# State-space blocks in a hybrid encoder: decay sums spread to all partitions by adding transfers instead of matmuls

## The chip, the core and the metric

The kernel runs on one core of a Trainium2 chip. The metric is the device time of one execution in microseconds (us). Before the change its median is 2278.6 us over 3 runs (2277.65 to 2280.53).

## What is computed

Two layers of an encoder are applied to two groups of tokens, 256 and 512 (768 tokens together), with width 1024. Each layer has a mixer (a Hyena convolution beside a Mamba-2 state-space scan), cross-attention into memory, and an MLP. The change lies in the state-space part of the mixer alone. What it must compute for each chunk of 128 tokens, cut to what matters:

```python
def segsum_exp(a):
    cs = jnp.cumsum(a, axis=-1)
    diff = cs[..., :, None] - cs[..., None, :]
    return jnp.where(mask, jnp.exp(jnp.where(mask, diff, 0.0)), 0.0)

Lmat = segsum_exp(dA)                               # per head, chunk and direction: 128 x 128
cb = jnp.einsum("bclgn,bcsgn->bgcls", Cc, Bc)       # per group of heads and chunk: 128 x 128
y_diag = jnp.einsum("bgrcls,bcsgrp->bclgrp", cb[:, :, None] * Lmat, xd)
```

There are 8 heads in 2 groups and 6 chunks of 128 tokens, so 12 blocks in a layer (block n: chunk n // 2, group n % 2). For each block and each of the two directions, the kernel needs exp(cs[l] - cs[s] + mask) for 4 heads: a tile of 128 partitions (s) by 4 x 128 (l). The term cs[l] must therefore stand on every partition: that is what "spread" means here.

## The kernel before, in words

Everything is in feature-major layout: 128 features on the partitions, 768 tokens along the row. All weights come from one stream of chunks in DRAM, 128 x 1024 each. TensorE works on float32 data as three products of rounded halves (high x high, low x high, high x low). A weight chunk is prepared by three engines: SyncE loads `raw`, ScalarE writes `wlo` = -raw and `whi` = rounded raw (`high_part`, L686 and L687), and GpSimd issues a DMA that adds the chunk from DRAM onto `wlo` (`low_halves`, L635). This is done in two halves of 512 columns. Each weight slot is used by every second tile.

The input projection is a run of 20 tiles per layer (`project(j)` on TensorE, through `tile`, L1346). A tile is 8 steps k of 6 matmuls, each over 384 tokens. A hook can put other products between two steps. Tiles 0 to 7 give the inputs of the scan, tiles 8 to 19 those of Hyena. Beside tiles 8 to 19 the 12 state-space blocks are worked, one beside each tile, in an order that each engine's own program writes out by hand:

- TensorE: `turn_cum` (L1452) transposes the cumulated sums after tile 8. `blocks(n)` writes C.B of the block into bank `MB[0]` (L1266) and, for both directions, the spread cs[l] into `MB[2]` and `MB[3]`: a matmul of a column of `group_r`, broadcast, against `wide` (L1271, and L1274 for block 0), added onto the mask that ScalarE laid into the bank. Block 0 has its mask from a matmul with `mask_r` (L1275). `blocks(0)` is in the middle of tile 9 (hook at k = 4), `blocks(n)` after tile 8+n. `diag(n)` (L1286, 8 small matmuls) multiplies the finished weights by the inputs, in the middle of tile 8+n+2. The last two, `diag(10)` and `diag(11)`, stand in the gate projection that follows (`beside_gate`, after its token tiles 1 and 4; L1309 to L1311).
- ScalarE, iteration j = 8+n: `high_part` of the chunk two tiles ahead (its first half can go from the middle of tile j, its second from the end), the copy of C.B into `cbs` (L785), 8 exponentials from the banks into `expd` (L789, buffer pair n % 2), then two masks for the next block into the banks (L795).
- VectorE: `project(8+n)` (two reads of the tile's bank, L2077 and L2078, which free it for tile j+2, then a convolution, L2081 and L2088 or L2085), `take(n-1)` (L2220 and L2222, the second reads what `diag(n-1)` wrote), and `weights(n)` (L2205 to L2210: four operations from `expd` to `wmat`, which `diag(n)` reads).
- GpSimd issues only the two `wlo` halves per tile in this stretch.

Ahead of that, VectorE copies three tables (L2176 to L2178), clears and fills `cum2` (L2179, L2185), and after the transposition makes `wide` (L2193, L2196).

Of the kernel before, what the change touches and what calls it, by code (L numbers as in the profile page):

```python
# [27 lines left out]
P = 128  # L28
# [45 lines left out]
LAST_DOWN = (DEPTH - 1) * CH + C_MLP  # L74
END_X, END_SQ, END_ACC = DEPTH * TILES - 6, DEPTH * 24 - 8, DEPTH * 24 - 7
# [25 lines left out]
CONST["group"] = CONST["g_first"] + 8  # L101
CONST["head"] = CONST["group"] + 12
CONST["stack"] = CONST["head"] + 4
# [60 lines left out]
def build_trunk(nc, xT, memT, wstream, dft, fw3, params, consts, x_kept, down_sum, yT):  # L164
    ctx = ExitStack()
    with ctx:
# [52 lines left out]
        expd = [place(f"expd{i}", [P, 4, P], oB + 36864 + 2048 * i) for i in range(4)]  # L219
# [8 lines left out]
        cum2 = place("cum2", [P, 2, P], oRING)  # L228
        cumT = place("cumT", [P, 2, P], oRING + 1024, F32R)
        wide = place("wide", [P, 2, 4, P], oRING + 2048, F32R)  # L230
        ident_r = place("ident_r", [P, P], oRING + 6144, F32R)
        mask_r = place("mask_r", [P, 2, P], oRING + 6656, F32R)
        group_r = place("group_r", [P, 12], oRING + 7680, F32R)
# [183 lines left out]
        tab_r, cum_t, cum_hi, wide_r = sem("rounded_tables"), sem("cum_turned"), sem("cum_hi"), sem("cum_spread")  # L417
# [208 lines left out]
        def _(pool):  # L626
# [10 lines left out]

            for L in range(DEPTH):
                for c in range(0 if L else AHEAD, C_MLP):
                    low_halves(L, c)  # L640
                w = L * STREAM + QUERY + C_MLP
# [37 lines left out]
        def _(act):  # L679
# [61 lines left out]
            for L in range(DEPTH):  # L741

                act.wait_ge(s_par, L * 16 + 16)
                act.activation(negA[:, :], par_("alog", 0, 16), ACT.Exp).then_inc(wdt_h, 1)
                for j in range(20):
                    if j == 8:
                        act.wait_ge(cum_t, L + 1)
                        act.activation(cumT[:, :, :], MB[2][:, 128:384].rearrange("p (d l) -> p d l", d=2),
                                       ACT.Copy).then_inc(cum_hi, 1)
# [29 lines left out]
                    if j >= 8:  # L779
# [6 lines left out]
                        t, g = n // 2, n % 2  # L786
                        for d in range(2):
                            for h in range(4):
                                ins = act.activation(expd[2 * (n % 2) + d][:, h, :], MB[2 + d][:, h * P:(h + 1) * P], ACT.Exp,  # L789
                                                     bias=ncum[:, d, t, 4 * g + h:4 * g + h + 1])  # L790
                            ins.then_inc(ssd_e, 1)
                        if n < 11:
                            act.wait_ge(ssd_e, L * 24 + 2 * n + 2)
                            for d in range(2):
                                act.activation(MB[2 + d].rearrange("p (h l) -> p h l", h=4),  # L795
                                               c_("maskf", 0, 2 * P).rearrange("p (d l) -> p d l", d=2)[:, d:d + 1, :].to_broadcast([P, 4, P]),
                                               ACT.Copy).then_inc(mask_in, 1)
# [456 lines left out]
        def blocks(pe, L, n):  # L1254

            t, g = n // 2, n % 2
            tk = slice(t * P, (t + 1) * P)
            if n:
                pe.wait_ge(cb_c, L * 12 + n)
                pe.wait_ge(ssd_e, L * 24 + 2 * n)  # L1260
            else:
                pe.wait_ge(wide_r, L * 2 + 2)
                pe.wait_ge(tab_r, L * 3 + 3)
                pe.wait_ge(x_c, L * 9 + 6)
                pe.wait_ge(silu_d, L * 16 + 16)
            pe.matmul(MB[0][:, 0:P], bcf[:, g, tk], bcf[:, 2 + g, tk], start=True, stop=True)  # L1266
            for d in range(2):
                out = MB[2 + d].rearrange("p (h l) -> p h l", h=4)
                if n:
                    pe.wait_ge(mask_in, L * 22 + 2 * (n - 1) + d + 1)  # L1270
                    last = pe.matmul(out, group_r[:, n:n + 1].to_broadcast([P, P]), wide[:, d, :, :], start=False, stop=True,  # L1271
                                     skip_group_check=True)
                    continue
                pe.matmul(out, group_r[:, n:n + 1].to_broadcast([P, P]), wide[:, d, :, :], start=True, stop=False)  # L1274
                last = pe.matmul(out, ident_r[:, :], mask_r[:, d:d + 1, :].to_broadcast([P, 4, P]), start=False, stop=True)  # L1275
            last.then_inc(ssd_mm, 1)
# [27 lines left out]
        def _(pe):  # L1304
# [67 lines left out]
            for L in range(DEPTH):  # L1372
# [75 lines left out]
                def turn_cum():  # L1448

                    pe.wait_ge(cum_c, L + 1)  # L1450
                    for d in range(2):
                        last = turn(MB[2][:, (d + 1) * P:(d + 2) * P], cum2[:, d, :], ident)  # L1452
                    last.then_inc(cum_t, 1)

                for n in range(TT * GROUPS):
                    project(8 + n, None, (lambda: diag(pe, L, n - 2)) if n >= 2 else (lambda: blocks(pe, L, 0)) if n else None)
                    if n == 0:
                        turn_cum()
                    else:
                        blocks(pe, L, n)  # L1460
# [33 lines left out]
                def beside_gate(u):  # L1494
# [3 lines left out]
                    elif u == 3:  # L1498
                        pe.wait_ge(ssd_e, L * 24 + 24)
# [464 lines left out]
        def _(dve):  # L1964
# [96 lines left out]
            for L in range(DEPTH):  # L2061
# [114 lines left out]
                dve.tensor_copy(ident_r[:, :], ident).then_inc(tab_r, 1)  # L2176
# [882 lines left out]
```

## Time and profile before

| | us |
|---|---|
| median of 3 runs | 2278.6 |
| the profiled execution, its time | 2277.9 |
| its span in the profile | 2276.0 |
| TensorE busy | 2255.4 (99%) |
| VectorE busy | 1612.0 (71%) |
| ScalarE busy | 1275.7 (56%) |
| GpSimd busy | 442.5 (19%) |

A busy share of 99% on TensorE means that the span is nearly the sum of what TensorE does, in its order. The other engines' shares are means over stages, and what counts for them is whether their work for a tile is ready when TensorE comes to it. The profile's page gives sums. The views of the trace used below are: who waited for whom, the groups of instructions by line, the stretches (busy time of each engine between two times), the instructions in order of time, and the DMA transfers with their time from issue to landing.

### The profile page before, as it was taken

The numbers are of one execution on the slowest core, as the hardware profiler recorded it, in microseconds if no ns is written. First come the engines' busy times: TensorE is split into PE (matmuls) and PEld (weight loads), VectorE is DVE, ScalarE is ACT, GpSimd is POOL, SyncE is SP. The second block draws the span as 40 slices with busy tenths as digits, with TensorE's granted clock in tenths as the row PEclk, the third lists the DMA queues.
The fourth block names the chain that finished last, engine by engine and source line by source line (L and its number), as shares of the span: only waits on it lengthen the run. The fifth ranks groups of instructions, "written<-read, shape, count | busy, mean of one in ns | idle before, by whom it ended". The sixth has DMA issues, their size and how long they took to land.

```text
span 2276.0 us, 33664 instructions
## 1 busy us (share of the span) xinstructions
PE 2255.4 (99%) x12336; PEld 2103.4 (92%) x12336; DVE 1612.0 (71%) x2671; ACT 1275.7 (56%) x2616; POOL 442.5 (19%) x512
## 2 busy tenths in 40 slices
PE   8999999999999999999999999999999999999998
PEld 7999779889899999999999996898989999999997
DVE  8888785365588867766679778745655888678566
ACT  5555445555466666666436545455555666666662
POOL 1111002310112232231211110023001122332320
PEclk9999999999999999999999999999999999999999
DMA  5554326852266696888655543278324665976984
GB/s 162 112 115 107 98 84 145 183 135 66 60 175 147 148 197 125 179 175 231 130 120 108 107 114 96 66 177 183 106 56 83 176 171 129 197 143 154 195 238 109
DMA packets 128705, 313.10 MB, mean 138 GB/s; under 512 B 14678, under 2 KB 28246, under 8 KB 128548
## 3 DMA queue, kind: packets, MB, share of 16 engines
q0 software_dynamic: 72128, 135.30, 34.5%
q1 hardware_dynamic: 55124, 173.62, 24.3%
q8 instruction: 97, 1.59, 0.3%
q10 hardware_dynamic: 1296, 2.10, 0.2%
q14 instruction: 60, 0.49, 0.1%
HBM read 276.36 MB, written 34.60 MB: 137 GB/s over the span
## 4 chain that ended last, share of the span: by engine, by line
PE 92%; DVE 4%; DMA 2%; ACT 2%; issue 1%; ACTq 0%; SPq 0%; POOL 0%; DVEq 0%
PE G L1346 28%; PE M L1865 9%; PE G L1865 8%; PE M L1876 6%; PE G L1876 6%; PE G L1913 2%; PE M L1881 2%; PE G L1881 2%; PE M L1870 2%; PE G L1870 2%; PE M L1309 2%; PE M L1311 2%; PE M L1310 2%; PE M L1346 1%; DVE tap L2088 1%; PE M L1575 1%
## 5 line engine op out<-in xcount | busy, mean ns | idle before, releaser
L635 POOL DMA_DIRECT2D wlo<-wstream x236 | 209.4, 888 | 1061.9 <-ACT wlo L686 890.1
L686 ACT ACTIVATE wlo<-raw 128x512 fp32r<-128x512 f32 x220 | 138.2, 628 | 305.3 <-PE G L1346 227.9
L1346 PE MATMUL G<-A_hi,whi 128*128 128x384 f32 x864 | 294.1, 340 | 9.3 <-DVE A_lo L2048 8.9
L1346 PE MATMUL G<-A_hi,wlo 128*128 128x384 f32 x864 | 290.1, 336 | 0.0
L648 POOL DMA_DIRECT2D w_low<-wstream x192 | 166.4, 870 | 615.1 <-ACT w_low L1063 615.1
L1346 PE MATMUL G<-A_lo,whi 128*128 128x384 f32 x864 | 285.3, 336 | 0.0
L1074 ACT ACTIVATE whi<-raw 128x384 fp32r<-128x384 f32 (+1 forms) x224 | 128.8, 575 | 117.7 <-DVE raw L2617 73.4
L1074 ACT ACTIVATE whi<-raw_b 128x384 fp32r<-128x384 f32 (+1 forms) x224 | 128.7, 575 | 111.0 <-DVE raw_b L2617 72.2
L1346 PEld LDWEIGHTS G<-A_hi,whi 128*128 128x128 f32 x864 | 163.4, 189 | 13.2 <-issue 11.2
L1346 PEld LDWEIGHTS G<-A_lo,whi 128*128 128x128 f32 x864 | 162.9, 189 | 1.0
L1346 PEld LDWEIGHTS G<-A_hi,wlo 128*128 128x128 f32 x864 | 163.1, 189 | 0.0
L687 ACT ACTIVATE whi<-raw 128x512 fp32r<-128x512 f32 x220 | 135.6, 616 | 0.0
L1346 PE MATMUL G<-B_hi,whi 128*128 128x384 f32 x352 | 117.6, 334 | 0.3 <-DVE B_lo L2663 0.3
L1346 PE MATMUL G<-B_lo,whi 128*128 128x384 f32 x352 | 117.6, 334 | 0.0
L1346 PE MATMUL G<-B_hi,wlo 128*128 128x384 f32 x352 | 117.6, 334 | 0.0
L2088 DVE SCALAR_TENSOR_TENSOR tap<-pad,par,tap 128x770 f32<-128x770 f32 x104 | 106.2, 1021 | 3.7
L2625 DVE TENSOR_TENSOR wlo<-raw,whi 128x384 fp32r<-128x384 f32 (+1 forms) x128 | 79.4, 622 | 40.4 <-ACT whi L1074 40.3
L2625 DVE TENSOR_TENSOR wlo<-raw_b,whi 128x384 fp32r<-128x384 f32 (+1 forms) x128 | 79.6, 622 | 38.3 <-ACT whi L1074 38.3
L2649 DVE TENSOR_TENSOR slice_lo<-slice_raw,slice_hi 128x384 fp32r<-128x384 f32 x168 | 90.7, 552 | 3.8 <-ACT slice_hi L1107 2.9
L1107 ACT ACTIVATE slice_hi<-slice_raw 128x384 fp32r<-128x384 f32 x168 | 86.2, 513 | 1.7 <-DVE slice_raw L2705 0.8
L1865 PE MATMUL G<-mlp_hi,whi 128*128 128x384 f32 x336 | 76.6, 335 | 1.1 <-ACT u_two L1137 1.1
L1865 PE MATMUL M<-mlp_hi,whi 128*128 128x384 f32 x336 | 76.4, 335 | 0.0
(555 smaller groups left out, 6160.5 us busy)
## 6 DMA issues: line engine op xcount, KB each, us to landing
raw<-wstream SPq DMA_DIRECT2D x172, 512.0 KB, 4.5
wlo<-wstream POOLq DMA_DIRECT2D x236, 256.0 KB, 5.4
w_low<-wstream POOLq DMA_DIRECT2D x96, 256.0 KB, 4.7
w_low<-wstream POOLq DMA_DIRECT2D x96, 192.0 KB, 4.0
down_sum<-staged POOLq DMA_DIRECT2D x48, 384.0 KB, 8.1
raw_b<-wstream SPq DMA_DIRECT2D x32, 512.0 KB, 7.3
raw_b<-wstream SPq DMA_DIRECT2D x32, 384.0 KB, 4.2
raw<-wstream SPq DMA_DIRECT2D x32, 384.0 KB, 4.2
```

The source lines that it names most:

```text
L635: pool.dma_start(low, wstream[stream(L, c)][:, part], accum_op=ALU.add).then_inc(lo_in[c % 2][h], 16)
L648: pool.dma_start(w_low[i][:, 0:n], wstream[w + 2 * f + row][:, col * n:(col + 1) * n], accum_op=ALU.add).then_inc(u_lo[i], 16)
L686: act.activation(wlo[:, s, part], raw[:, s, part], ACT.Copy, scale=-1.0).then_inc(neg_done, 1)
L687: act.activation(whi[:, s, part], raw[:, s, part], ACT.Copy).then_inc(hi_done, 1)
L1074: act.activation(whi[:, s, part.start:part.start + width(f)], quad(f, *QUADS[n]), ACT.Copy).then_inc(u_hi, 1)
L1346: last = mm(out, w, p[:, k, a:b], start=(k == 0 and w is w_hi and p is parts[0]), stop=(k == KT - 1 and (w is w_lo and only is None or onl ...
L1865: mm(out, high(k), src(i, k), start=(not added and k == 0 and i == 0), stop=False, skip_group_check=added)
L1870: mm(out, high(end), src(0, end), start=False, stop=False, skip_group_check=added)
L1876: mm(out, low(k), src(0, k), start=False, stop=False, skip_group_check=added)
L1881: mm(out, high(end), src(1, end), start=False, stop=True, skip_group_check=added).then_inc(u_mm, 1)
L2088: ins = stt(out=dst[:, 0:n], in0=p[:, first + k:first + k + n], scalar=w(k), in1=dst[:, 0:n], op0=ALU.mult, op1=ALU.add)
L2625: tt(wlo[:, s, where], src, f_(whi[:, s, where]), ALU.subtract).then_inc(u_dlo, 1)
```

## The change

The matmuls that spread cs[l] are gone. TensorE transposes the cumulated sums `cum` themselves (48 rows per direction), in tile 8 ahead of k = 7. ScalarE copies the rows to `cum_rows` and stores them in DRAM (`cum_kept`) with two DMAs. For each block ScalarE now lays the two masks into `expd` in SBUF, in three buffer pairs (n % 3), and GpSimd issues two DMAs that add four rows (4 x 128 values, 2 KB) from DRAM, the same for all 128 partitions, onto them (`spread`). The exponentials are then taken in place in `expd` (`exps_of`), once both transfers have landed. `SPREADS` says behind which weight chunk on GpSimd's queue each block's pair of transfers stands. In iteration n ScalarE takes the exponentials of block n and lays the masks of block n+1; at the start it is shifted: iteration 0 lays mask 0, iteration 1 takes exponentials 0 and lays masks 1 and 2, iteration 2 takes exponentials 1 and 2 and lays mask 3. VectorE accordingly makes weights 0 after its work on tile 9, weights 1 and 2 after its work on tile 10, and takes block 1 ahead of its work on tile 11. TensorE does `diag(0)` in tile 11 and `diag(1)` and `diag(2)` in tile 12 (k = 1 and k = 5); from block 3 on its order is the old one. The tables `ident_r`, `mask_r`, `group_r`, and `cum2`, `cumT` and `wide`, with the VectorE work that fills them, are gone.

The diff, cut to its core:

```diff
@@ -72,6 +72,7 @@
 LAST_DOWN = (DEPTH - 1) * CH + C_MLP
+SPREADS = {10: (0,), 11: (1, 2), **{c: (c - 9,) for c in range(12, 21)}}
 END_X, END_SQ, END_ACC = DEPTH * TILES - 6, DEPTH * 24 - 8, DEPTH * 24 - 7
...
@@ -216,7 +215,7 @@
         xsf = place("xsf", [P, 4, T], oB + 36864)
-        expd = [place(f"expd{i}", [P, 4, P], oB + 36864 + 2048 * i) for i in range(4)]
+        expd = [place(f"expd{i}", [P, 4, P], oB + 36864 + 2048 * i if i < 4 else oRING + 2048 * (i - 3)) for i in range(6)]
         wmat = [place(f"wmat{i}", [P, 4, P], oB + 36864 + 8192 + 2048 * i) for i in range(2)]
...
@@ -225,12 +224,7 @@
         wxh, wxl = place("wxh", [P, D], oRING, F32R), place("wxl", [P, D], oRING + 4096, F32R)
-        cum2 = place("cum2", [P, 2, P], oRING)
-        cumT = place("cumT", [P, 2, P], oRING + 1024, F32R)
-        wide = place("wide", [P, 2, 4, P], oRING + 2048, F32R)
-        ident_r = place("ident_r", [P, P], oRING + 6144, F32R)
-        mask_r = place("mask_r", [P, 2, P], oRING + 6656, F32R)
-        group_r = place("group_r", [P, 12], oRING + 7680, F32R)
+        cum_rows = place("cum_rows", [P, 2, P], oRING)
         ncum = place("ncum", [P, 2, TT, HEADS], oRING + 7744)
...
@@ -635,9 +630,23 @@
+            def spread(L, n):
+                t, g = n // 2, n % 2
+                if n == 0:
+                    pool.wait_ge(cum_out, 32 * (L + 1))
+                for d in range(2):
+                    pool.wait_ge(mask_in, L * 24 + 2 * n + d + 1)
+                    rows = cum_kept[L, d, t * HEADS + 4 * g:t * HEADS + 4 * g + 4, :]
+                    pool.dma_start(expd[2 * (n % 3) + d][:, :, :].rearrange("p h l -> p (h l)"),
+                                   rows.rearrange("(o h) l -> o (h l)", o=1).to_broadcast([P, 4 * P]),
+                                   accum_op=ALU.add).then_inc(cum_s[n % 3], 16)
             for L in range(DEPTH):
                 for c in range(0 if L else AHEAD, C_MLP):
                     low_halves(L, c)
+                    for n in SPREADS.get(c, ()):
+                        spread(L, n)
                 w = L * STREAM + QUERY + C_MLP
...
@@ -742,11 +751,31 @@
                 act.activation(negA[:, :], par_("alog", 0, 16), ACT.Exp).then_inc(wdt_h, 1)
+                def exps_of(n):
+                    t, g = n // 2, n % 2
+                    act.wait_ge(cum_s[n % 3], 32 * (L * 4 + n // 3 + 1))
+                    for d in range(2):
+                        for h in range(4):
+                            e = expd[2 * (n % 3) + d][:, h, :]
+                            ins = act.activation(e, e, ACT.Exp, bias=ncum[:, d, t, 4 * g + h:4 * g + h + 1])
+                        ins.then_inc(ssd_e, 1)
+                def lay_mask(n):
+                    for d in range(2):
+                        act.activation(expd[2 * (n % 3) + d][:, :, :],
+                                       c_("maskf", 0, 2 * P).rearrange("p (d l) -> p d l", d=2)[:, d:d + 1, :].to_broadcast([P, 4, P]),
+                                       ACT.Copy).then_inc(mask_in, 1)
                 for j in range(20):
                     if j == 8:
                         act.wait_ge(cum_t, L + 1)
-                        act.activation(cumT[:, :, :], MB[2][:, 128:384].rearrange("p (d l) -> p d l", d=2),
-                                       ACT.Copy).then_inc(cum_hi, 1)
+                        act.activation(cum_rows[0:48, :, :], MB[2][0:48, 128:384].rearrange("p (d l) -> p d l", d=2),
+                                       ACT.Copy).then_inc(cum_r, 1)
+                        act.wait_ge(cum_r, L + 1)
+                        for d in range(2):
+                            act.dma_start(cum_kept[L, d], cum_rows[0:48, d, :]).then_inc(cum_out, 16)
                     if j not in (1, 2):
...
@@ -783,18 +812,13 @@
                         act.activation(cbs[:, n % 2, :], MB[0][:, 0:P], ACT.Copy).then_inc(cb_c, 1)
-                        t, g = n // 2, n % 2
-                        for d in range(2):
-                            for h in range(4):
-                                ins = act.activation(expd[2 * (n % 2) + d][:, h, :], MB[2 + d][:, h * P:(h + 1) * P], ACT.Exp,
-                                                     bias=ncum[:, d, t, 4 * g + h:4 * g + h + 1])
-                            ins.then_inc(ssd_e, 1)
-                        if n < 11:
-                            act.wait_ge(ssd_e, L * 24 + 2 * n + 2)
-                            for d in range(2):
-                                act.activation(MB[2 + d].rearrange("p (h l) -> p h l", h=4),
-                                               c_("maskf", 0, 2 * P).rearrange("p (d l) -> p d l", d=2)[:, d:d + 1, :].to_broadcast([P, 4, P]),
-                                               ACT.Copy).then_inc(mask_in, 1)
+                        for e in ((), (0,), (1, 2))[n] if n < 3 else (n,):
+                            exps_of(e)
+                        for m in ((0,), (1, 2), (3,))[n] if n < 3 else (n + 1,):
+                            if 3 <= m < TT * GROUPS:
+                                act.wait_ge(ssd_w, L * 12 + (m - 2))
+                            if m < TT * GROUPS:
+                                lay_mask(m)
                 def copy_b(i):
...
@@ -1257,23 +1281,10 @@
                 pe.wait_ge(cb_c, L * 12 + n)
-                pe.wait_ge(ssd_e, L * 24 + 2 * n)
             else:
-                pe.wait_ge(wide_r, L * 2 + 2)
-                pe.wait_ge(tab_r, L * 3 + 3)
                 pe.wait_ge(x_c, L * 9 + 6)
                 pe.wait_ge(silu_d, L * 16 + 16)
-            pe.matmul(MB[0][:, 0:P], bcf[:, g, tk], bcf[:, 2 + g, tk], start=True, stop=True)
-            for d in range(2):
-                out = MB[2 + d].rearrange("p (h l) -> p h l", h=4)
-                if n:
-                    pe.wait_ge(mask_in, L * 22 + 2 * (n - 1) + d + 1)
-                    last = pe.matmul(out, group_r[:, n:n + 1].to_broadcast([P, P]), wide[:, d, :, :], start=False, stop=True,
-                                     skip_group_check=True)
-                    continue
-                pe.matmul(out, group_r[:, n:n + 1].to_broadcast([P, P]), wide[:, d, :, :], start=True, stop=False)
-                last = pe.matmul(out, ident_r[:, :], mask_r[:, d:d + 1, :].to_broadcast([P, 4, P]), start=False, stop=True)
-            last.then_inc(ssd_mm, 1)
+            pe.matmul(MB[0][:, 0:P], bcf[:, g, tk], bcf[:, 2 + g, tk], start=True, stop=True).then_inc(ssd_mm, 1)
...
@@ -1449,14 +1460,21 @@
                     for d in range(2):
-                        last = turn(MB[2][:, (d + 1) * P:(d + 2) * P], cum2[:, d, :], ident)
+                        last = turn(MB[2][0:48, (d + 1) * P:(d + 2) * P], cum[:, d, :, :].rearrange("p c h -> p (c h)"), ident)
                     last.then_inc(cum_t, 1)
                 for n in range(TT * GROUPS):
-                    project(8 + n, None, (lambda: diag(pe, L, n - 2)) if n >= 2 else (lambda: blocks(pe, L, 0)) if n else None)
+                    diags = iter({0: (), 1: (), 2: (), 3: (0,), 4: (1, 2)}.get(n, (n - 2,)))
                     if n == 0:
-                        turn_cum()
+                        hook, hook_at = turn_cum, (7,)
+                    elif n == 1:
+                        hook, hook_at = (lambda: blocks(pe, L, 0)), (4,)
+                    elif n == 2:
+                        hook, hook_at = None, None
                     else:
+                        hook, hook_at = (lambda: diag(pe, L, next(diags))), ((1, 5) if n == 4 else (4,))
+                    project(8 + n, None, hook, hook_at)
+                    if n:
                         blocks(pe, L, n)
...
@@ -1495,8 +1513,6 @@
                         diag(pe, L, TT * GROUPS - 2)
-                    elif u == 3:
-                        pe.wait_ge(ssd_e, L * 24 + 24)
                     elif u == 4:
...
@@ -2173,33 +2189,19 @@
                 flat = lambda a: a[:, :, :, :].rearrange("p d c h -> p (d c h)")
-                dve.tensor_copy(ident_r[:, :], ident).then_inc(tab_r, 1)
-                dve.tensor_copy(mask_r[:, :, :].rearrange("p d l -> p (d l)"), c_("maskf", 0, 2 * P)).then_inc(tab_r, 1)
-                dve.tensor_copy(group_r[:, :], c_("group", 0, 12)).then_inc(tab_r, 1)
-                link(dve.memset(cum2[:, :, :], 0.0))
                 project(6)
                 project(7)
                 dve.wait_ge(cum_mm, L + 1)
-                for d in range(2):
-                    for part in range(2):
-                        link(dve.tensor_copy(cum2[:, d, part * 64:part * 64 + 48], MB[2][:, d * 48:(d + 1) * 48]))
                 link(dve.tensor_copy(flat(cum), MB[2][:, 0:96]))
                 link(ts(flat(ncum), flat(cum), -1.0, None, ALU.mult))
                 link(tt(flat(wst), MB[3][:, 0:96], flat(cum), ALU.subtract))
                 dve.tensor_copy(flat(dec), MB[3][:, 0:96]).then_inc(cum_c, 1)
                 dve.wait_ge(cum_c, L + 1)
-                dve.wait_ge(cum_hi, L + 1)
-                link(tt(cumT[64:128, :, :], MB[2][64:128, 128:384].rearrange("p (d l) -> p d l", d=2), f_(cumT[64:128, :, :]),
-                        ALU.subtract))
-                for d in range(2):
-                    tt(wide[:, d, :, :], f_(cumT[:, d:d + 1, :]).to_broadcast([P, 4, P]),
-                       c_("head", 0, 4).rearrange("p (h l) -> p h l", l=1).to_broadcast([P, 4, P]), ALU.mult).then_inc(wide_r, 1)
-
                 def weights(n):
                     t, g = n // 2, n % 2
-                    e0, e1 = expd[2 * (n % 2)], expd[2 * (n % 2) + 1]
+                    e0, e1 = expd[2 * (n % 3)], expd[2 * (n % 3) + 1]
...
@@ -2222,10 +2224,18 @@
                 for n in range(12):
+                    if n == 3:
+                        take(1)
                     project(8 + n)
-                    if n:
+                    if n == 1:
+                        weights(0)
+                    elif n == 2:
+                        take(0)
+                        weights(1)
+                        weights(2)
+                    elif n > 2:
                         take(n - 1)
-                    weights(n)
+                        weights(n)
                 take(11)
...
```

## Rows read from the trace of the kernel before

**Rows 1.** The profile's page, busy time, share, instructions.
```profile
PE 2255.4 (99%) x12336; PEld 2103.4 (92%) x12336; DVE 1612.0 (71%) x2671; ACT 1275.7 (56%) x2616; POOL 442.5 (19%) x512
```

**Rows 2.** Waits of TensorE, whole span: waiter, releaser, us, times, longest.
```profile
PE G L1346 <- DVE A_lo L2048: 8.9, 1, 8.9
```

**Rows 3.** Tiles 8 to 19: window, length, busy PE PEld DVE ACT POOL, clock, DMA.
```profile
101.50:211.40 109.90, 109.90 (x664) 108.75 (x663) 87.64 (x134) 64.00 (x169) 22.04 (x23) 1.00 0.52 108
1228.50:1338.20 109.70, 109.70 (x663) 108.55 (x662) 87.67 (x134) 64.50 (x172) 21.63 (x23) 1.00 0.52 109
```

**Rows 4.** Groups by line on TensorE: count, busy us, mean ns, idle before.
```profile
L1271 PE MATMUL M<-wide,group_r 128*128 128x512 f32 x44 | 15.6, 436 | 0.0
```

**Rows 5.** TensorE in order of time, layer 0: start, us, what.
```profile
101.75 0.38 PE L1452 MATMUL M<-cst,cum 128*128 128x128 f32 x2
101.89 0.42 PE L1346 MATMUL G<-A_hi,whi 128*128 128x384 f32 x1
102.15 0.33 PE L1346 MATMUL G<-A_lo,whi 128*128 128x384 f32 x1
102.32 0.34 PE L1346 MATMUL G<-A_hi,wlo 128*128 128x384 f32 x1
...
106.16 0.38 PE L1266 MATMUL M<-bcf 128*128 128x128 f32 x2
...
107.31 0.34 PE L1346 MATMUL G<-A_hi,whi 128*128 128x384 f32 x1
...
111.50 0.38 PE L1266 MATMUL M<-bcf 128*128 128x128 f32 x2
...
112.18 0.33 PE L1346 MATMUL G<-A_hi,whi 128*128 128x384 f32 x1
...
122.10 0.33 PE L1346 MATMUL G<-A_hi,whi 128*128 128x384 f32 x1
```

**Rows 6.** VectorE for tile 11, layer 0: start, us, what, idle before.
```profile
131.61 0.42 DVE L2077 TENSOR_TENSOR pad<-G,rbc 128x256 f32<-128x256 f32 x1 [1.01 <-PE G L1346]
...
139.82 0.69 DVE L2210 TENSOR_TENSOR wmat<-expd,sq 128x512 f32<-128x512 f32 x1
```

**Rows 7.** VectorE at tile 19 and block 11, layer 0.
```profile
210.97 0.43 DVE L2077 TENSOR_TENSOR pad<-G,rbc 128x256 f32<-128x256 f32 x1 [1.02 <-PE G L1346]
...
216.16 0.68 DVE L2205 TENSOR_TENSOR expd<-expd,dt__67 128x512 f32<-128x512 f32 x1
...
218.33 0.69 DVE L2210 TENSOR_TENSOR wmat<-expd,sq 128x512 f32<-128x512 f32 x1
```

**Rows 8.** Layer 0, line 1286 (`diag`), 200 to 222 us: what it waited for.
```profile
  DVE wmat L2210: 0.2, 1
```

**Rows 9.** ScalarE, iteration of tile 10, layer 0: exponentials, masks, next weight half.
```profile
122.83 2.17 ACT L789 ACTIVATE expd<-M,ncum 128x128 f32<-128x128 f32 x8
125.03 1.12 ACT L795 ACTIVATE M<-cst 128x512 f32<-128x512 f32 x2
126.54 0.63 ACT L686 ACTIVATE wlo<-raw 128x512 fp32r<-128x512 f32 x1 [0.39 <-PE G L1346]
```

**Rows 10.** GpSimd's issues of adding transfers, layer 0: start, us, idle before.
```profile
104.41 0.87 POOL L635 DMA_DIRECT2D wlo<-wstream  x1 [0.18 <-issue]
...
122.54 1.16 POOL L635 DMA_DIRECT2D wlo<-wstream  x1 [4.13 <-ACT wlo L686]
127.47 0.87 POOL L635 DMA_DIRECT2D wlo<-wstream  x1 [3.76 <-ACT wlo L686]
```

**Rows 11.** DMA, 101.5 to 211.4 us: GpSimd's queue, and issues to landing (median).
```profile
q0 software_dynamic: 3314, 6.03, 32.8%
...
wlo<-wstream POOLq DMA_DIRECT2D x23, 256.0 KB, 4.3
```

**Rows 12.** Line 635 over the whole span, from issue to landing.
```profile
DMA to landing us min/median/max: 3.6/5.4/9.8
```

**Rows 13.** ScalarE's queue at the start of the kernel: a DMA issue.
```profile
0.76 0.41 ACTq L726 DMA_DIRECT2D X<-xT  x1
```

More of the change, by code:

```diff
@@ L100 @@
 CONST["g_first"] = CONST["alt"] + 1
-CONST["group"] = CONST["g_first"] + 8
-CONST["head"] = CONST["group"] + 12
-CONST["stack"] = CONST["head"] + 4
+CONST["stack"] = CONST["g_first"] + 8
 CONST["eps"] = CONST["stack"] + 16
@@ L161, with build_trunk @@
 SCRATCH = 4096
-def build_trunk(nc, xT, memT, wstream, dft, fw3, params, consts, x_kept, down_sum, yT):
+def build_trunk(nc, xT, memT, wstream, dft, fw3, params, consts, cum_kept, x_kept, down_sum, yT):
     ctx = ExitStack()
@@ L416, in build_trunk @@
         mask_in = sem("mask_laid")
-        tab_r, cum_t, cum_hi, wide_r = sem("rounded_tables"), sem("cum_turned"), sem("cum_hi"), sem("cum_spread")
+        cum_t, cum_r, cum_out = sem("cum_turned"), sem("cum_rows_copied"), sem("cum_rows_out")
+        cum_s = [sem(f"cum_spread{i}") for i in range(3)]
         ssd_mm, cb_c, ssd_e, ssd_w, ssd_y = (sem(n) for n in (
@@ L2901, in constants @@
     out[:, CONST["g_first"]:CONST["g_first"] + KT] = i["norm_mix"][0].reshape(KT, P).T
-    row = np.arange(P) % 64
-    used = row < 48
-    out[used, CONST["group"] + row[used] // 4] = 1
-    out[used, CONST["head"] + row[used] % 4] = 1
     rows = np.arange(P)
@@ L3051 @@
     args = [nc.dram_tensor(n, a.shape, F32, kind="ExternalInput").ap() for n, a in arrays.items()]
+    cum_kept = nc.dram_tensor("cum_kept", (DEPTH, 2, TT * HEADS, P), F32, kind="Internal").ap()
     x_kept = nc.dram_tensor("x_kept", (KT, P, T), F32, kind="Internal").ap()
@@ L3054 @@
     yT = nc.dram_tensor("yT", (D, T), F32, kind="ExternalOutput").ap()
-    build_trunk(nc, *args, x_kept, down_sum, yT)
+    build_trunk(nc, *args, cum_kept, x_kept, down_sum, yT)
     r = run_bass_kernel_spmd(nc, [arrays], core_ids=[0])
```

## The prediction

> **What bounds the kernel now.** I read the page's busy times first: TensorE 2255.4 us of 2276.0, 99% [rows 1]. Then its waits: the one long wait is 8.9 us at the start, no other reaches 1.2 us in total, and none lies in the run of tiles that is changed [rows 2]. Then the two stretches that hold tiles 8 to 19: TensorE is busy for all of 109.9 and 109.7 us, at full granted clock, VectorE for 87.6, ScalarE for 64.0, GpSimd for 22.0, and the DMA engines are busy 0.52 of the time [rows 3]. So in these stretches time is gained only by taking products off TensorE, and it is lost again as soon as another engine hands something over late. The sum is made against the profiled execution, 2277.9 us; the median of the runs, 2278.6, is 0.7 above it, and I add that at the end.
>
> **Removed from TensorE.** The group for L1271 has 44 matmuls with 15.6 us of busy time [rows 4], but busy times of pipelined matmuls overlap, so I go by starts. Block 1: the C.B product starts at 111.50, the next tile's first product at 112.18, so the block takes 0.68 us [rows 5]. What stays is the C.B product, a pair of 128x128. The transposition, also such a pair, shows its price: it starts at 101.75, the next product at 101.89, and the one after it 0.26 later, where the usual step is 0.17: 0.14 + 0.09 = 0.23 us [rows 5]. Saved: 0.45 us for each of blocks 1 to 11. Block 0, with four matmuls, takes 107.31 - 106.16 = 1.15 us; saved 0.92 [rows 5]. A layer: 11 x 0.45 + 0.92 = 5.9; both layers 11.7 us. The transposition keeps its price. The tile from 112.18 to 122.10 lasts 9.92 us [rows 5] and will last 9.47.
>
> **VectorE.** The tables, `cum2` and `wide` go, nothing is added. It was not on the path, so this gains nothing by itself. For tile 11 it works from 131.61 to 140.51 (139.82 + 0.69), 8.9 us [rows 6]: it still fits a tile of 9.47, and is 0.57 from being the bound. One place has no such room: for block 11 it starts on the tile at 210.97 and ends the last weights at 219.02 [rows 7], and TensorE already waited 0.2 us for just that [rows 8]. This chain starts at the end of tile 19 and is not shortened, while TensorE comes to `diag(11)` 0.45 us earlier, because block 11's matmuls are gone. That saving is a new wait: -0.45 per layer, 0.9 in all. I take it for both layers.
>
> **ScalarE.** The exponentials read SBUF instead of PSUM and the masks are written to SBUF; the trace has no such form with these operands, but ScalarE is idle for 0.4 of the stretch [rows 3], so a price of ±20% on 3.3 us per block moves only the lap below. The two stores of the rows cost two issues, some 0.41 us each by the only such rows [rows 13], ahead of the weight half for tile 10. Before, that half was issued one step ahead of the second one at 104.41 [rows 10], so at 103.4, and with 4.3 us to landing [rows 11] lay ready at 107.7; tile 10 will start near 110.8. A delay of 0.8 is covered, with 5.4 to landing too; without that cover it would cost at most 0.8 per layer. The transposition is one step k earlier, about 1 us, which pays for it.
>
> **GpSimd and the transfers: the price that decides.** 24 adding transfers of 256 KB are added per layer, two per block. Queued on GpSimd behind their waits (for the rows in DRAM, and for the masks) are the `wlo` halves; a half issued at 127.47 [rows 10] is for the tile that starts two tiles after 122.10 [rows 5], at 141.9, so it can bear some us. 23 such transfers took 32.8% of 109.9 us of the 16 engines, 1.57 us each [rows 11]; 24 more raise the DMA share from 0.52 to about 0.88. It fits, barely.
> The transfers stand in a lap that was not there: exponentials of n, masks of n+1, transfers, exponentials of n+1. Its length [rows 9, 10]: masks start 2.20 us after the exponentials (125.03 - 122.83); the first mask is done after 0.56; GpSimd reacts in 0.30 (127.47 - 127.17, the end of the half at 126.54); its issue takes 0.87, the gap 0.18, so the second transfer is issued at 4.11. With 4.3 us to landing [rows 11], plus 0.5 because a transfer takes 1.57 and the issues are 1.05 apart, the lap is 8.9 us. A tile is 9.47. It closes with 0.55 to spare, as long as the second transfer lands within 5.36 us.
> Bounds: the same kind of transfer took 3.6 at the least, 5.4 as a median over the whole kernel, 9.8 at the most [rows 12]. I take 4.3 (4.8 for the second), the median of just this stretch, with the same size, queue and weight traffic beside it; no reason excludes the other ends, above all since all 128 partitions read one 2 KB row, a pattern that has no row.
> The start makes a lag. Four transfers for blocks 1 and 2 go out together; counted from exponentials 0, the fourth lands at 3.06 + 4.3 + 3 x 1.57 = 12.1, exponentials 2 end at 14.3, and transfer 3 lands 6.7 later, at 21.0. Without a lag it would be two tiles, 8.6 + 9.47 = 18.0. So block 3 is 3.0 us late, up to 4.6 with weight halves between. The laps win 0.55 each, 4.4 over eight blocks. Cover: `diag(n)` comes 13.6 us after its tile's end and weights take 2.9, so exponentials may be 7 us late without cost. Only block 11 has little: VectorE turns to its weights 5.2 us after tile 19's end [rows 7], exponentials without a lag end 3.6 after it, so 1.6 are free. At 4.3 the lag is gone by then.
>
> The Trainium skill, page DMA: Bandwidth & Descriptors, section Anatomy of one DMA, puts such a transfer at about 2.0 us plus its bytes over 436 GB/s; my estimate from that is 2.6 us for 256 KB. The trace does not agree: no such transfer took under 3.6 [rows 12]. By the page the lap would be near 7 us and the lag would vanish sooner.
>
> **Sum.** 11.7 - 0.9 = 10.8 us gained: 2277.9 - 10.8 = 2267.1 in the profiled execution, 2267.8 as a median.
>
> **Rivals.**
> A. The lap is about as long as a tile (second transfer at 5.1 to 5.6 us). At 5.1, 0.26 is won per lap, 2.1 in all, and 3.0 of about 5 remain: a further wait of 1.4 per layer at `diag(11)`, 2271. At 5.36 nothing is won: 5.5 - 1.6 = 3.9 per layer, 2276. For it: the 5.4 [rows 12]. Against it: the 4.3 [rows 11].
> B. Slower: the broadcast transfer is slow, the lap beats the tile. Place: TensorE before `diag`, growing with each block. Price per layer: 4.4 (the 3.9 of A and the 0.45 above) plus about 10 times the excess over 5.36 (eight laps, and the start). It breaks even at 5.5 and is slower by 0.2% from 5.7; 7 us gives 2 x (4.4 + 16.4) - 11.7 = 30 lost, 2309; 9.8 gives 2365. For it: the DMA engines would be near 0.9 busy, and nothing shows what one row read 128 times does. Against it: the transfer has the same size and the same rows of 2 KB at its destination.
> C. Descriptors are late. GpSimd's issue took 0.87 alone but 1.16 beside VectorE's work [rows 10]. If both issues of each pair take 1.16, the lap is 9.5 and wins nothing: 4.6 + 0.6 - 1.6 = 3.6 per layer, 2275. The Trainium skill, page SBUF: State Buffer, section A bandwidth-pool intuition that's wrong, says that VectorE can lock GpSimd out while it writes descriptors, and gives 620 ns alone against 3100 ns; the trace agrees in sign only, its worst issue beside VectorE being 1.16. By that factor this would end as B does.
> D. The change does what it says but TensorE's time is refilled: VectorE, at 8.9 of 9.47, is later than I count (convolutions slowed by the traffic). Then tiles keep 9.92 and only block 0's saving, 1.8 us, is left: 2277.
>
> **How the numbers follow.** About 0.2%, 4.6 us, is what a measurement of this kernel can tell from no change: faster is below 2274.0, slower above 2283.2. Forecast (lap closes, 2266 to 2269): 0.60. A: 0.12, two thirds of it faster. B: 0.15, nearly all slower. C: 0.07, D: 0.06, both within 0.2%. So faster 0.68, same 0.17, slower 0.15. The low end is the full saving without the wait at block 11, and 1 us for the slow steps after each block that I left out: 2265. The high end takes in A, C, D and the first of B: 2281. For the forecast alone: 2265.5 to 2269.5.
>
> **What would show it.** Right: no L1271 on TensorE; tiles 10 to 18 at 9.47 (start to start); TensorE waits only about half a us at L1286 for `wmat` in each layer; ScalarE waits for the transfers ahead of exponentials 1 to 3, less with each block. Wrong: transfers onto `expd` that land after more than 5.4 us, ScalarE waits before the exponentials that do not shrink, TensorE waits at L1286 in every tile. The prediction falls most easily with that one unmeasured duration.

## The result and the profile after

| | before | after |
|---|---|---|
| median of the runs, us | 2278.1 (2277.5 to 2280.5) | 2302.5 (2300.7 to 2302.8) |
| ratio to before | | 1.0106 [1.0093, 1.0119] |
| span of the profiled execution, us | 2276.0 | 2300.3 |
| waits of TensorE in tiles 8 to 19 and block 11, both layers, us | 0.2 [rows 8] | 27.6 |

The change makes the kernel 24.4 us slower; forecast were 10.8 us gained. The page of after, its busy times, the chain that ended last by engines, and the new transfers (count, size, median from issue to landing):

```profile
span 2300.3 us, 33570 instructions
PE 2252.5 (98%) x12284; PEld 2099.0 (91%) x12284; DVE 1607.6 (70%) x2649; ACT 1280.5 (56%) x2620; POOL 482.3 (21%) x560
...
PE 80%; DMA 9%; ACT 4%; DVE 4%; issue 1%; POOL 1%; SPq 0%; ACTq 0%; DVEq 0%
...
expd<-cum_kept POOLq DMA_DIRECT2D x48, 256.0 KB, 5.9
```

TensorE has 52 matmuls fewer than in [rows 1], and is busy for hardly less: 2252.5 against 2255.4. The chain now runs through transfers for 9% of the span; before it was 2%. Next the waits of TensorE over the whole span (total, times, longest), the answer to [rows 2]:

```profile
PE G L1357 <- DMA wlo<-wstream: 18.4, 13, 3.2
PE G L1357 <- DVE A_lo L2064: 8.7, 1, 8.7
PE M L1297 <- DVE wmat L2212: 6.4, 2, 3.3
PE G L1320 <- DMA wlo<-wstream: 3.2, 2, 2.3
```

L1357 is the first product of a tile (L1346 before), L1297 is `diag` (L1286 before), L1320 a product of the gate. The 8.7 us were there before, at the start. Nearly all the rest is new: 21.6 us for low weight halves at the start of tiles, and 6.4 for the weights of block 11, one wait in each layer.

Where the halves went is seen on ScalarE and GpSimd, one iteration of layer 0 (start, length, what, idle before it and what ended that); it answers [rows 9, 10]:

```profile
151.12 2.45 ACT L761 ACTIVATE expd<-expd,ncum 128x128 f32<-128x128 f32 x8 [4.64 <-DMA expd<-cum_kept]
153.47 1.14 ACT L767 ACTIVATE expd<-cst 128x512 f32<-128x512 f32 x2
154.52 0.61 ACT L695 ACTIVATE wlo<-raw 128x512 fp32r<-128x512 f32 x1
155.04 0.61 ACT L696 ACTIVATE whi<-raw 128x512 fp32r<-128x512 f32 x1
155.56 0.61 ACT L695 ACTIVATE wlo<-raw 128x512 fp32r<-128x512 f32 x1
...
161.15 2.45 ACT L761 ACTIVATE expd<-expd,ncum 128x128 f32<-128x128 f32 x8 [4.30 <-DMA expd<-cum_kept]
```
```profile
154.38 1.75 POOL L641 DMA_DIRECT2D expd<-cum_kept  x2 [6.83 <-ACT expd L767]
155.45 2.47 POOL L630 DMA_DIRECT2D wlo<-wstream  x2
```

Exponentials wait for their transfers, masks follow them, then both weight halves of a coming tile at once; on GpSimd the two spreads and both halves leave in one burst. The row of the spreads merges two issues; here the second of them, and its time from issue to landing:

```profile
154.92 1.22 POOL L641 DMA_DIRECT2D expd<-cum_kept  x1
...
expd<-cum_kept POOLq DMA_DIRECT2D x1, 256.0 KB, 6.2
```

It is issued 154.92 - 151.12 = 3.80 us after the exponentials, and lands as the next ones start. From exponentials to exponentials are 161.15 - 151.12 = 10.03 us. Over the eight laps from block 3 (140.74) to block 11 (223.89) the mean is 10.39, one of them 12.46; in layer 1 it is (1363.02 - 1279.29) / 8 = 10.47. TensorE's tile, with its waits, follows: from the C.B product at 142.27 to that at 216.89 are seven tiles, 10.66 us each in the mean. The transfers in the window from 142 to 217 us, the answer to [rows 11]:

```profile
q0 software_dynamic: 4059, 7.40, 62.0%
...
expd<-cum_kept POOLq DMA_DIRECT2D x14, 256.0 KB, 5.2
wlo<-wstream POOLq DMA_DIRECT2D x14, 256.0 KB, 9.0
raw<-wstream SPq DMA_DIRECT2D x7, 512.0 KB, 7.9
```

A low half took 4.3 us to land and takes 9.0. The halves issued from 155.45 are for the tile that starts at 162.55, and its first product comes at 164.58, 9.1 later. TensorE in order of time, three tile starts and `diag(11)`:

```profile
130.46 0.41 PE L1357 MATMUL G<-A_hi,whi 128*128 128x384 f32 x1 [3.20 <-DMA wlo<-wstream]
...
153.23 0.41 PE L1357 MATMUL G<-A_hi,whi 128*128 128x384 f32 x1 [1.11 <-DMA wlo<-wstream]
...
164.58 0.41 PE L1357 MATMUL G<-A_hi,whi 128*128 128x384 f32 x1 [1.64 <-DMA wlo<-wstream]
...
229.30 0.95 PE L1297 MATMUL M<-xtok,wmat 128*128 128x64 f32 x6 [3.09 <-DVE wmat L2212]
```

The waits are not all. After the wait of 3.20 us the same products run slower; here the stretch behind it, and two windows (length, busy PE PEld DVE ACT POOL, granted clock, DMA share, GB/s):

```profile
131.10 0.52 PE L1357 MATMUL G<-A_hi,whi 128*128 128x384 f32 x1
131.42 0.52 PE L1357 MATMUL G<-A_lo,whi 128*128 128x384 f32 x1
...
134.59 0.34 PE L1357 MATMUL G<-A_hi,whi 128*128 128x384 f32 x1
134.77 0.34 PE L1357 MATMUL G<-A_lo,whi 128*128 128x384 f32 x1
```
```profile
130.00:140.00 10.00, 9.54 (x51) 9.57 (x52) 8.39 (x14) 4.65 (x12) 3.57 (x4) 0.83 0.60 116
140.00:150.00 10.00, 10.00 (x63) 10.00 (x62) 7.68 (x12) 5.74 (x15) 3.54 (x4) 1.00 0.66 106
```

The step from product to product is 0.32 instead of 0.18 for some 3 us: the lower of TensorE's two levels, 1.2 instead of 2.4 GHz, behind a stretch in which the engine stood idle. It happens twice per layer, behind the waits of 3.20 and 3.09 us in layer 0, and of 2.51 and 3.31 in layer 1; a mean clock of 0.83 over 10 us is 1.7 us lost, four times 6.8.

### The profile page after: what moved, and what is told of

It reads as the page before. It is cut to its first block, busy times and chain, and to the rows that moved or that the text cites. A ratio compares the mean times of both kernels' runs of the same rounds, so it can differ in the third digit from the quotient of the medians.

```text
span 2300.3 us, 33570 instructions
## 1 busy us (share of the span) xinstructions
PE 2252.5 (98%) x12284; PEld 2099.0 (91%) x12284; DVE 1607.6 (70%) x2649; ACT 1280.5 (56%) x2620; POOL 482.3 (21%) x560
## 4 chain that ended last, share of the span: by engine, by line
PE 80%; DMA 9%; ACT 4%; DVE 4%; issue 1%; POOL 1%; SPq 0%; ACTq 0%; DVEq 0%
PE G L1357 20%; PE M L1881 8%; PE G L1881 8%; DMA expd<-cum_kept 7%; PE M L1892 6%; PE G L1892 5%; PE G L1929 3%; ACT expd L761 2%; PE M L1897 2%; PE G L1897 2%; PE M L1886 2%; PE G L1886 2%; PE M L1322 2%; PE M L1320 2%; PE M L1321 2%; DVE tap L2104 1%
## 5 line engine op out<-in xcount | busy, mean ns | idle before, releaser
L630 POOL DMA_DIRECT2D wlo<-wstream x236 | 222.4, 1000 | 898.0 <-ACT wlo L695 728.0
L1357 PE MATMUL G<-A_hi,whi 128*128 128x384 f32 x864 | 296.9, 344 | 27.5 <-DMA wlo<-wstream 18.4
L1357 PE MATMUL G<-A_hi,wlo 128*128 128x384 f32 x864 | 290.8, 337 | 0.0
L1357 PE MATMUL G<-A_lo,whi 128*128 128x384 f32 x864 | 286.0, 337 | 0.0
L1357 PEld LDWEIGHTS G<-A_hi,whi 128*128 128x128 f32 x864 | 163.8, 190 | 32.8 <-issue 31.6
L1357 PEld LDWEIGHTS G<-A_hi,wlo 128*128 128x128 f32 x864 | 163.6, 189 | 0.0
L1357 PEld LDWEIGHTS G<-A_lo,whi 128*128 128x128 f32 x864 | 163.4, 190 | 0.1
L1357 PE MATMUL G<-B_hi,whi 128*128 128x384 f32 x352 | 117.7, 334 | 0.0
L1357 PE MATMUL G<-B_hi,wlo 128*128 128x384 f32 x352 | 117.6, 334 | 0.0
L1357 PE MATMUL G<-B_lo,whi 128*128 128x384 f32 x352 | 117.6, 334 | 0.0
L761 ACT ACTIVATE expd<-expd,ncum 128x128 f32<-128x128 f32 x192 | 58.8, 389 | 104.0 <-DMA expd<-cum_kept 104.0
```

The source lines that it names most:

```text
L630: pool.dma_start(low, wstream[stream(L, c)][:, part], accum_op=ALU.add).then_inc(lo_in[c % 2][h], 16)
L761: ins = act.activation(e, e, ACT.Exp, bias=ncum[:, d, t, 4 * g + h:4 * g + h + 1])
L1357: last = mm(out, w, p[:, k, a:b], start=(k == 0 and w is w_hi and p is parts[0]), stop=(k == KT - 1 and (w is w_lo and only is None or onl ...
```

## The experiments

**Masks first.** The order on ScalarE alone: the masks of the next block ahead of this block's exponentials. Same work, transfers and traffic.

```diff
-                        for e in ((), (0,), (1, 2))[n] if n < 3 else (n,):
-                            exps_of(e)
                         for m in ((0,), (1, 2), (3,))[n] if n < 3 else (n + 1,):
                             ...
+                        for e in ((), (0,), (1, 2))[n] if n < 3 else (n,):
+                            exps_of(e)
```

> The changed kernel with one edit: in each of ScalarE's iterations the masks of the next block are laid ahead of this block's exponentials, not behind them (the third buffer pair is free by then). Nothing is left out. Theory LAP (the loss comes from a lap exponentials, masks, transfers, exponentials of about 10.0 us against a tile of 9.47, which also holds up the weight halves behind it on ScalarE): the lap is cut, tiles 12 to 18 come back to 9.47, 2266 to 2272 us. Theory TRAFFIC (24 more transfers of 256 KB per layer make the weight halves land late wherever they are issued): the weight halves still land at 9 us, 2290 to 2302. Theory ROW (reading one 2 KB row 128 times is slow): transfers still take about 6 us from issue to landing, but they are covered: 2266 to 2275, so this run alone doesn't tell ROW from LAP.

Measured: 2265.0 us, ratio to before 0.9943 [0.9927, 0.9960]; 37.5 us below after, and faster than both kernels. ScalarE no longer stands before the exponentials, and GpSimd's burst is apart; below, ScalarE and GpSimd in order of time, then the transfers from 142 to 217 us:

```profile
149.04 1.14 ACT L767 ACTIVATE expd<-cst 128x512 f32<-128x512 f32 x2
150.08 2.44 ACT L761 ACTIVATE expd<-expd,ncum 128x128 f32<-128x128 f32 x8
...
159.55 2.44 ACT L761 ACTIVATE expd<-expd,ncum 128x128 f32<-128x128 f32 x8
```
```profile
149.95 1.76 POOL L641 DMA_DIRECT2D expd<-cum_kept  x2
153.33 0.87 POOL L630 DMA_DIRECT2D wlo<-wstream  x1 [1.62 <-ACT wlo L695]
158.21 1.10 POOL L630 DMA_DIRECT2D wlo<-wstream  x1 [4.01 <-ACT wlo L695]
```
```profile
wlo<-wstream POOLq DMA_DIRECT2D x15, 256.0 KB, 6.1
raw<-wstream SPq DMA_DIRECT2D x7, 512.0 KB, 4.3
expd<-cum_kept POOLq DMA_DIRECT2D x13, 256.0 KB, 6.9
```

The iteration is 9.47 us. The adding transfers take longer than in after, 6.9 against 5.2, and it costs nothing: the transfers for block n+1 now have a whole tile until the exponentials of n+1. TensorE's only new wait in layer 0 is 0.4 us at `diag(11)`. So it is the lap, not the duration of a transfer by itself.

**Own rows.** Each partition adds its own row of the weight stream in place of the one row that all read.

```diff
-                                   rows.rearrange("(o h) l -> o (h l)", o=1).to_broadcast([P, 4 * P]),
+                                   wstream[2 * n + d][:, 0:4 * P],
```

> The changed kernel, but each adding transfer reads 128 different rows of 2 KB (from the weight stream) instead of one row for all partitions; the decay sums are therefore not added and the exponentials use the sum itself as bias, so the state-space outputs are not the reference's. Same count, size, order and waits. Theory ROW: transfers land as the weight halves did before, 4.3 us (second about 4.8), lap 8.9, 2266 to 2275 us. Theories LAP and TRAFFIC: nothing changes, 2298 to 2305, landing median 5.9.

Measured: 2315.6 us, 1.0165 [1.0148, 1.0182], slower than after. The laps are longer too (139.51 to 150.86 and 162.97: 11.3 and 12.1 us; the mean of eight is 11.35 in layer 0 and 11.07 in layer 1, against 10.39 and 10.47). One row for 128 partitions is not what is slow; of the two it is the faster.

**No transfers.** The adding transfers are left out, with the exponentials on unfinished sums.

```diff
+                    continue
                     rows = cum_kept[L, d, t * HEADS + 4 * g:t * HEADS + 4 * g + 4, :]
```

> The changed kernel without the 24 adding transfers of each layer; ScalarE waits only for the masks, and the decay sums are not added (bias is the sum itself), so the state-space outputs are not the reference's. Rows are still stored. All theories: only what was taken off TensorE is left, minus the wait at the last block: 2266 to 2269 us by the sum of the prediction (11.7 saved, 0.9 given back). If it is above 2272, part of the loss has another cause than the transfers.

Measured: 2265.1 us, 0.9943 [0.9927, 0.9960]. That is all that the rest of the change is worth, 12.5 us. In profiled executions (2265.8 against 2300.3, 34.5 apart) the balance closes: TensorE is idle 25.8 us more in after (2300.3 - 2252.5 against 2265.8 - 2243.8), and the same 12284 matmuls are busy 2252.5 instead of 2243.8 us, 8.7 more, of which the lower clock is 6.8.

**Transfers beside.** The same adding transfers with the same source, onto two buffers that nothing reads. ScalarE waits for none.

```diff
-                    pool.dma_start(expd[2 * (n % 3) + d][:, :, :].rearrange("p h l -> p (h l)"),
+                    if L or n:
+                        pool.wait_ge(cum_s[d], 16 * (L * 12 + n))
+                    pool.dma_start(beside[d][:, :],
```

> As the kernel without transfers (the decay sums are not added, outputs not the reference's), but the 24 transfers per layer are issued at the same places of GpSimd's queue onto a buffer that nobody reads; only the next transfer of the same direction waits for the last one's landing. Same DMA traffic, no lap through ScalarE. Theory LAP: 2266 to 2270 us, as without transfers. Theory TRAFFIC: most of the loss stays, 2288 to 2302. Theory ROW: as LAP here.

Measured: 2269.4 us, 0.9961 [0.9947, 0.9975], 4.3 above the kernel without transfers; the intervals overlap. From 142 to 217 us these transfers land in 5.1 us in the median, as in after (5.2). The profiled execution is the slowest of five, 2275.4 us. In it TensorE waits for a low half once in each layer, 1.9 and 1.6 us, and behind both the lower clock shows again (granted 0.83 from 130 to 140 and from 1256 to 1266 us). The traffic by itself costs some 4 us; the other 33 us of after's loss need ScalarE's wait.

**One direction.** One transfer per block instead of two.

```diff
+                    if d:
+                        continue
                     rows = cum_kept[L, d, t * HEADS + 4 * g:t * HEADS + 4 * g + 4, :]
```

> The changed kernel with one adding transfer per block instead of two: the backward direction gets its mask but no decay sums (its bias is the sum itself), so the state-space outputs are not the reference's. Theory LAP: 2.35 us of exponentials, 0.91 to the first issue, and one transfer of 3.9 to 4.4 us make a lap of 7.2 to 7.7, under the tile of 9.47: the whole loss goes, 2264 to 2269 us. Theory TRAFFIC (the loss follows the bytes added): half of it goes, 2280 to 2290.

Measured: 2265.8 us, 0.9946 [0.9929, 0.9962]. Transfers land in 4.7 us; with no second issue the lap would be 8.0 (3.26 to the first issue, as in after, and 4.7), and from block 4 on the exponentials wait for nothing. A lap below the tile costs nothing, as the theory has it.

**One half ahead.** To ask whether only the weight halves hold TensorE: the first half of the next tile is prepared and issued ahead of exponentials, masks and spreads.

```diff
+                        if j < 19:
+                            high_part(L, C_IN + j + 1, (0,))
                         for e in ((), (0,), (1, 2))[n] if n < 3 else (n,):
                             exps_of(e)
```

> The changed kernel, nothing left out; the lap stays, but the first weight half of the next tile is taken out of it: ScalarE prepares it ahead of the block's exponentials and GpSimd issues it ahead of the block's transfers. Theory A (the prediction's cover was wrong because the weight halves stood behind the lap, and with them there TensorE pays every late lap at once): its waits for weight halves at the start of a tile shrink to near nothing, the lag of the laps only shows at the last block, 2 x 8 us, 2278 to 2287. Theory B (TensorE is held by the lap itself, wherever the halves stand): 2296 to 2305.

Measured: 2337.9 us, 1.0261 [1.0244, 1.0278]. Both expectations missed the time. Waits of TensorE in layer 0, from 98 to 240 us:

```profile
PE M L1303 <- DVE wmat L2218: 16.9, 8, 3.3
PE G L1326 <- DMA wlo<-wstream: 0.3, 1, 0.3
```

The halves are no longer waited for, as meant, but `diag` (L1303) now waits in most tiles, at the pace of the lap, which is (240.70 - 141.58) / 8 = 12.39 us long. Over the whole span these are 45.0 us in 19 waits, the longest, 6.4 and 6.9, at block 11. So the halves were only the first thing that the lap held up; freed of them TensorE is held by the weights of `diag`. Why the lap grew by 2 us is not settled. Exponentials to the first issue still take 3.27 us; from there to the next exponentials it is 8.74 (157.05 to 165.79) instead of 6.77, so the transfers land later. SP's load of `raw` is issued 1.44 us behind the first spread (158.49) instead of 2.48 (156.86 against 154.38), and could be what shares the engines with the second spread; no run took that apart.

**A longer lap, twice.** Two extra writes of 512 columns on ScalarE, 1.05 us, ahead of each block's masks: once in after, once with the masks first.

```diff
                 def lay_mask(n):
 
+                    act.wait_ge(mask_in, L * 24 + 2 * n)
+                    for d in range(2):
+                        act.activation(longer[d][:, :, :], ...)
```

> The changed kernel with ScalarE writing two more tiles of the masks' size (1.05 us together) ahead of each block's masks, onto a buffer that nobody reads: the lap is 1.05 us longer, the transfers are the same, ScalarE is still idle for a third of the stretch. Theory LAP: 1.05 for each of some 10 laps in each layer, 2318 to 2325 us. Theory TRAFFIC: hidden in ScalarE's idle time, 2300 to 2305.

> The same two extra writes per block, in the kernel that lays the masks ahead of the exponentials. Theory LAP: there is no lap to lengthen, 2264 to 2268 us, as without them (2265.0). If ScalarE's work itself were what holds the tiles, it would rise by 15 us or more.

Measured: 2328.6 us, 1.0232 [1.0210, 1.0255], in after; 2265.0 us, 0.9940 [0.9923, 0.9957], with the masks first. The same microsecond costs 26 us in the one order and nothing in the other. In the first the mean lap of layer 0 is (236.31 - 144.34) / 8 = 11.50, 1.11 more than the 10.39 of after, and that of layer 1 (1386.98 - 1292.37) / 8 = 11.83, 1.36 more. Eight laps of each are 19.8 us. In the profiled executions, 23.3 apart, TensorE is idle 11.8 us more and busy 11.5 more (2264.0), which fits more time at the lower clock (mean granted clock 0.989 against 0.995). The expectation, 2318 to 2325, had the lap right in the main, and came out some 4 us low; what makes them up is not settled.

**One half ahead, masks first.** The edit of one half ahead, in the kernel with the masks first.

> The earlier weight half of the kernel with one half ahead, in the kernel that lays the masks ahead of the exponentials. In the kernel with one half ahead TensorE waited for the weights of diag, 23.3 and 14.9 us, and the time was 2337.9. Theory LAP (those waits come through the lap that ScalarE's order closes, exponentials, masks, transfers): with the masks first there is no such lap, no long wait in the stretch, 2263 to 2268. Theory ORDER (an earlier half is costly by itself, because two weight halves and two adding transfers then stand in another order on ScalarE and GpSimd, or are twice in flight): TensorE still waits at diag or at the tile starts, 2285 to 2330.

Measured: 2277.3 us, 0.9997 [0.9987, 1.0006]. Between the two theories: of the 72.9 us from 2337.9 down to 2265.0, 60.6 go with the lap. The other 12.3 belong to the half: ScalarE waits 3.10 us for TensorE to release its buffer, ahead of masks and exponentials, which start 6.8 us behind the block's C.B product instead of 2.5 (156.31 - 149.54; with the masks first alone 150.08 - 147.62). In the middle of the stretch that costs nothing, the tile stays at 9.47. TensorE waits at `diag` three times in each layer, twice near the start (0.2 and 1.0 us) and at block 11 (2.4), and is busy 5.9 us more (2248.4 against 2242.5). The row is that of the whole span:

```profile
PE M L1303 <- DVE wmat L2218: 7.3, 6, 2.4
```

## Why the prediction was wrong

**Right.** The saving on TensorE. Tiles that nothing disturbs take 9.47 us (the C.B products at 142.27 and 151.74), as forecast, and the kernel without transfers gains 12.5 where the sum said 10.8. The wait at `diag(11)`, forecast to grow by 0.45 in each layer, is 0.4 there and with the masks first, in layer 0 alone. VectorE, 8.9 us per tile, fits into 9.47 (rival D is out). ScalarE's stores cost nothing that shows. GpSimd's two issues of a pair start 0.54 us apart (154.38 and 154.92) and take 1.75 together, where the sum had 1.05 from start to start. Over the kernel an issue took 1.09 in the median and 1.94 at most, nothing like the 3100 ns that rival C took from the Trainium skill, page SBUF: State Buffer, section A bandwidth-pool intuition that's wrong.

**The lap: mechanism right, the landing too small.** Exponentials to masks took 2.35 (153.47 - 151.12) where 2.20 was counted, masks to the first issue 0.91 where 0.86 was. The second transfer is issued at 3.80, against 4.11, and landed 6.2 later (10.03 - 3.80), where 4.8 was taken. The lap is 10.03 where the sum had 8.9 and the tile needs 9.47. The term that failed is the landing, which I took from a stretch in which GpSimd had half as many transfers. The answer was in the text, as bounds: 5.4 as median of the kernel [rows 12], 9.8 at the most, and the tipping point at 5.36. The raised DMA share was worked out too, but the landing was not raised with it.

**The start: the same term again.** Exponentials 3 come 26.6 us after exponentials 0 (140.74 - 114.12), where 21.0 was counted. Without transfers it is 18.0 (128.75 - 110.71), as the prediction had it, so block 3 is 8.6 us late, not 3.0 to 4.6. The last of the four transfers for blocks 1 and 2 landed 14.8 us after exponentials 0 (128.92 - 114.12) instead of 12.1. Exponentials 0 are late as well, by their own transfers: they start 9.7 us behind their C.B product (114.12 - 104.43), and 5.8 without transfers (110.71 - 104.88). That is not in the sum. Counted from C.B product 0, exponentials 11 of layer 0 are 19.0 us late (223.89 - 104.43 against 205.37 - 104.88). No lap wins anything back.

**The cover: wrong for the weight halves.** Rival B's own formula gives 2 x (4.4 + 10 x 0.92) - 11.7 = 15.5 us lost with the mean lap of 10.39; 24.4 were. The start, later than B had it, can make up the rest; no run took the two apart. B put the waits at `diag`, where "exponentials may be 7 us late without cost". They came at the starts of tiles. I had let the low halves off with "it can bear some us", by a half issued 14.4 us ahead of its tile. But each half stands on ScalarE behind the exponentials and on GpSimd behind the spreads, so it inherits their lateness; both halves then go at once, beside the SP queue's 512 KB load (`raw`, 7.9 us), and land in 9.0. Issue and first product are 9.1 us apart, so nothing is left. The 7 us of `diag` itself stand: exponentials 5 are 8.0 us later behind their C.B product than without transfers (161.15 - 151.74 against 148.57 - 147.15), TensorE gives 1.64 of it back by its wait ahead of that tile, and `diag(5)` does not wait; of all blocks only `diag(11)` does. So the cover decided where TensorE waits. How much it loses follows the lap: with one half ahead the waits moved to `diag`, and with the longer lap the loss grew.

**Left out: the clock.** Behind two long waits in each layer TensorE ran at its lower level, 6.8 us in all. No term of the sum and no rival had it; B's price counted waits alone. It need not come on top of them in full: while the lap holds the tiles, slower products can take the place of waiting. After the drop at 131 us the next tile, from 142.27 on, starts without a wait.

**The broadcast.** Rival B blamed the row that 128 partitions read. The direction was B's, the culprit not: own rows were slower still.

The Trainium skill, page DMA: Bandwidth & Descriptors, section Queues, rings and completion order, says that each engine of the 16 takes turns between the queues that have work for it. The trace is in line with it, though it does not prove it: the SP queue's load, on a queue of its own, lands in 7.9 us in after and in 4.3 with the masks first, when GpSimd's burst is spread out.

**Open.** What made one lap in layer 0 take 12.46 us, and the laps with one half ahead 12.39: in both the transfers land later, and the reason is only guessed at. And 1.9 of the 8.7 us of longer busy time are not tied to a place.

## What to carry to other kernels

When an engine waits for a transfer and then, in its own order, produces what the next transfer needs, there is a lap, and it runs beside the tile like a second clock: work out its length with the landing under the new traffic, and if it is near the tile, put the producing step ahead of the waiting one. Here two lines exchanged were worth 37.5 us, and turned a loss of 1.1% into a gain of 0.6%. Cover has to be worked out for everything queued behind the new wait, on that engine and on the next queue, and not for the consumer alone; it tells where the waits will show. It does not help for long against a lap longer than the tile: here the tile took the lap's length whichever consumer waited.

## What the runs showed of the hardware

Adding transfers of 256 KB on GpSimd's queue landed in 4.3 us at 0.52 DMA share [rows 3, 11], 5.2 in pairs in after (6.2 for the second of the pair shown), 6.9 with the masks first, and 9.0 for the last two of a burst of four. 128 partitions reading one 2 KB row were no slower than 128 own rows: landing 5.9 and 5.8 us over the kernel, but with own rows the mean laps were 0.95 and 0.60 us longer in the two layers. In after, waits of 2.51 to 3.31 us on TensorE were each followed by some microseconds at the lower clock, 1.7 us lost, and waits of 2.40 us and less in the same stretches were not. But with the transfers beside, waits of 1.9 and 1.6 us were followed by it too (granted 0.83 over 10 us), so the length of a single wait does not decide it.
